# Expert activations: the high part's products with both token parts as one product of 512 columns, the two halves summed on VectorE

## The chip, the cores and the metric

The kernel runs on one core of one Trainium2 chip. The metric is the device time of one execution in microseconds (us). It computes everything in fp32 precision; where a product is large, each fp32 operand is split into a high part (rounded to the type fp32r, which TensorE multiplies in one pass) and a low part (the remainder, also as fp32r), and the product is the sum of high by high, high by low, and low by high.

## What is computed

Two blocks one after the other, each with two layers, over 256 tokens of width 1024. The second block (attention of three kinds, and a wide MLP) is not touched. The first block ends each layer with a mixture of 16384 small experts, and that is where the change lies:

```python
q = (ht @ w_q).reshape(n_tok, PEER_HEADS, PEER_QDIM)
...
gate = jax.nn.softmax(top, axis=-1)
...
u = expert_u[ec]
act = jax.nn.gelu(jnp.einsum('td,thkd->thk', hc, u), approximate=False)
return jnp.einsum('thk,thkd->td', gc * act, expert_v[ec])
```

Each token chooses 16 experts in each of 8 heads out of 128 x 128. The kernel does it densely: it goes through the experts in 128 groups of 128 (called experts 0 to 127 below, index i), computes the activation of all 256 tokens for all 128 members, applies GELU, multiplies by a table of gates that is zero where a token did not choose the member, and adds the product with `expert_v` to an accumulator that holds all tokens.

## The kernel before, in words

**One expert group i** takes these operations, all in the loop of the expert stage:

- SyncE loads `expert_u` (128x1024) and `expert_v` (128x1024), two places each, well ahead.
- ScalarE `u_high` (L1762) rounds u to its high part `utr[:, m % 2, 0]`; VectorE `u_low` (L2456) subtracts and writes the low part `utr[:, m % 2, 1]`.
- TensorE `activations` (L1207): 8 slices k of the width, 3 products each (`HALVES`, L32), 24 products of 128x128 by 128x256 into 256 columns of a PSUM bank, `prob_ps[:, m % 2]`.
- ScalarE `gelu` (L1769) reads the bank and writes `ga[:, m % 2]` (128x256).
- VectorE `weighted` (L2470, L2472, L2474) multiplies by the gate's row, rounds to `wtr` high, subtracts for `wtr` low; the semaphore `wt_ready` follows.
- ScalarE `v_high` (L1779) and VectorE `v_low` (L2481) split v in the same way into `vr`, of which there is only one buffer, so that `v_high` waits for the end of the combine before (`v_used`).
- TensorE `combine` (L1219): 12 products of 128x512, accumulated into `acc`.

**The order of the work** is written out by hand and each engine keeps to its own: TensorE does activations(i), combine(i-1), activations(i+1), combine(i). ScalarE does u_high(i+1), gelu(i), v_high(i). VectorE does u_low(i+1), weighted(i), v_low(i). Combine(i) waits for `wt_ready` and for v_low(i). `prob_ps` has two banks used in turn; activations(i) waits until the GELU of i-2 has read its bank.

**The two layers** differ. In layer 1 the first 8 groups have their activations computed earlier (`EARLY`), from plain fp32, with GELU applied then; so 120 groups go through `activations`, 128 in layer 0: 248 in all. In layer 0, beside groups 27 to 122, the kernel also computes the modulation vectors of the next layer: a loop of 12 rounds of 8 groups, where VectorE, in the first four steps of each round, adds one "ada piece" between weighted(i) and v_low(i): two multiply-adds of 128x512 (`ada_piece`, L2129, called at L2514). One product on TensorE (L1263) and one copy on ScalarE (L1596) per round belong to it. The other groups of layer 0 and all of layer 1 have plain steps.

```python
for j in range(8):
    i = it * 8 + (PLAIN + 3 + j)
    u_low(i + 1, j)
    weighted(i, (3 + j) % 4)
    if j < 4:
        ...
        ada_piece(it + ADA_START, j, next_pieces, next_sum, next_row)
    ...
    v_low(i, (3 + j) % 4)
```

Of the kernel before, what the change touches and what calls it, by code (L numbers as in the profile page):

```python
# [11 lines left out]
ALU = mybir.AluOpType  # L12
ACT = mybir.ActivationFunctionType
X = mybir.AxisListType.X

P = 128
D = 1024
S = 256
T = S // P
KD = D // P  # L20
# [9 lines left out]
NKEYS = 128  # L30
PLACES = 2
HALVES = ((0, 0), (0, 1), (1, 0))  # L32
# [26 lines left out]
EARLY = (0, 8)  # L59
# [160 lines left out]
def two_blocks(nc, io, out):  # L220
    ctx = ExitStack()
    with ctx:
        def sem(name):
            return ctx.enter_context(nc.semaphore(name))
# [6 lines left out]
        prob_ps = ctx.enter_context(nc.psum_tensor("prob_ps", [P, 2, 512], F32))  # L231
# [60 lines left out]
        ut_act = Signal(sem("ut_act"), a=NKEYS)  # L292
        ut_dve = Signal(sem("ut_dve"), a=NKEYS)
        am_full = Signal(sem("am_full"), a=NKEYS)
        gelu_done = Signal(sem("gelu_done"), a=NKEYS)
        wt_ready = Signal(sem("wt_ready"), a=NKEYS)
        v_used = Signal(sem("v_used"), a=NKEYS)
# [39 lines left out]
        with ExitStack() as second:  # L337
# [4 lines left out]
            hTr = half("hTr", [P, 2, KD, S])  # L342
            wtr = half("wtr", [P, 2, 2, S])
            half("beside_experts", [P, 4096], F32)
            utr = half("utr", [P, 2, 2, D])
# [66 lines left out]
        start = Region(arena, start_at)  # L412
# [24 lines left out]
        ga = rc.take(2, S)  # L437
# [388 lines left out]
        def _(pe):  # L826
# [168 lines left out]
            for l in range(DEPTH):  # L995
# [40 lines left out]
                for t in range(T):  # L1036
                    for k in range(KD):
                        pe.matmul(acc[:, b, t, :], hT[:, k, t * P:t * P + P], w(k, 0, 256),
                                  start=(k == 0), stop=(k == KD - 1))
                for j in range(2):  # L1040
                    ins = columns_T(acc[:, b, 2 + j, :], w, hT, 256 + j * P)
# [9 lines left out]
                for t in range(T):  # L1051
                    for k in range(KD):
                        ins = pe.matmul(acc[:, b, t, :], hT[:, k, t * P:t * P + P], w(k, 0, 256),
                                        start=(k == 0), stop=(k == KD - 1))
# [12 lines left out]
                for g in range(4):  # L1067
                    r = 64 * (g % 2)
                    for kt in range(T):
                        ins = pe.matmul(pooled[r:r + 64, g // 2, :], z[:, kt, 768 + 64 * g:832 + 64 * g],  # L1070
                                        pool_m[:, kt, g, :], start=(kt == 0), stop=(kt == 1))
# [7 lines left out]
                for g in range(4):  # L1079
                    r = 64 * (g % 2)  # L1080
                    ins = pe.matmul(pooled[r:r + 64, g // 2, :], pool_wt[r:r + 64, g // 2, :],
                                    plT[r:r + 64, g // 2, :], start=True, stop=True)
# [63 lines left out]
                if l == 0:  # L1146
                    pe.wait_ge(t5_skew, 16 * 16)
                    pe.wait_ge(t5_kept, 1)
                    for h in range(8):
                        if h >= 2:  # L1150
                            pe.wait_ge(t5_done, h - 1)
                        pe.matmul(prob_ps[:, h % 2, :], flip, skewed[:, h].rearrange("p t s -> p (t s)"),
                                  start=True, stop=False)
                        pe.matmul(prob_ps[:, h % 2, :], ident[:], causal_a, start=False, stop=True).then_inc(t5_flip, 1)
                    pe.wait_ge(t5_done, 8)
                    for s in (7, 8):
                        pe.wait_ge(bias_row_in, 16 * s)
                        pe.matmul(prob_ps[:, (s - 1) % 2], ones, bias_row, start=True, stop=False)
                        for p in range(4):
                            pe.wait_ge(piece_in[p], s * 16 + 16)  # L1160
                            for k in range(2):
                                ins = pe.matmul(prob_ps[:, (s - 1) % 2], cbc[:, 2 * p + k, :], start_pieces[:, p, k],
                                                start=False, stop=(p == 3 and k == 1))
# [3 lines left out]
                for i in range(EARLY[l]):  # L1167
# [3 lines left out]
                    for k in range(KD):  # L1171
                        ins = pe.matmul(prob_ps[:, i % 2, 0:S], early_u[:, i, k * P:k * P + P], hT[:, k, :],
                                        start=(k == 0), stop=(k == KD - 1))
# [9 lines left out]
                for n in range(S // TOKG):  # L1183
# [5 lines left out]
                    for q in range(TOKG):  # L1189
                        ins = pe.matmul(gate_ps[:, n % 2, q * P:q * P + P], rows[:, n % 2, 1, q, :], rows[:, n % 2, 0, q, :],  # L1190
                                        start=True, stop=True)
# [5 lines left out]
                def activations(i, m):  # L1197

                    pe.wait_ge(*ut_act.at("a", l, i + 1 - EARLY[l]))
                    pe.wait_ge(*ut_dve.at("a", l, i + 1 - EARLY[l]))  # L1200
                    if not (isinstance(i, int) and i < EARLY[l] + 2):
                        pe.wait_ge(*gelu_done.at("a", l, i - 1 - EARLY[l]))
                    elif EARLY[l]:
                        pe.wait_ge(early_done, EARLY[l])
                    for k in range(KD):
                        for n, (uh, hh) in enumerate(HALVES):
                            ins = pe.matmul(prob_ps[:, m % 2, 0:S], utr[:, m % 2, uh, k * P:k * P + P], hTr[:, hh, k, :],  # L1207
                                            start=(k == 0 and n == 0), stop=(k == KD - 1 and n == 2))
                    ins.then_inc(am_full.sem, 1)

                def combine(i, m, first=False, last=False):
# [39 lines left out]
                else:  # L1251
# [3 lines left out]
                    with pe.Fori(0, 12) as it:  # L1255
                        for j in range(8):
                            i = it * 8 + (PLAIN + 3 + j)
# [15 lines left out]
            for l in range(DEPTH):  # L1273
# [42 lines left out]
                for i, (a, n) in enumerate(((0, 512), (512, 256))):  # L1316
# [3 lines left out]
                    for t in range(T):  # L1320
                        for k in range(2):
                            ins = pe.matmul(dst[:, t, 0:n], cqT[:, k, t * P:t * P + P], wuq[:, k, a:a + n],
                                            start=(k == 0), stop=(k == 1))
                    ins.then_inc(accs.full_sem("b", use), 1)
                proj_nat(l, "g1", "g1")
                for i in range(2):
# [3 lines left out]
                    for t in range(T):  # L1330
                        ins = pe.matmul(dst[:, t, :], ckvT[:, t * P:t * P + P], ob[:, i, 2 * BW:3 * BW],
                                        start=True, stop=True)
# [59 lines left out]
                for n in range(GC):  # L1392
# [3 lines left out]
                    for h in range(2):  # L1396
                        pe.wait_ge(*late_lo.at("b", l, 2 * NB + 2 * n + h + 1))
                        for t in range(T):
                            for k in range(4):
                                for m, (wp, hp) in enumerate(HALVES):  # L1400
                                    ins = pe.matmul(dst[:, t, :], (hT_hi, mx_lo)[hp][:, 4 * h + k, t * P:t * P + P],  # L1401
                                                    late_operand(2 * NB + 2 * n + h, wp)[:, k, :],
                                                    start=(h == 0 and k == 0 and m == 0), stop=(h == 1 and k == 3 and m == 2))
# [4 lines left out]
                for i in range(8):  # L1408
                    use = f"up{i}"
                    pe.wait_ge(*accs.free_at("b", l, use))  # L1410
                    for h in range(2):
# [3 lines left out]
                        for j in range(2):  # L1415
                            for n, (wp, hp) in enumerate(HALVES):
                                if j == 0 and n == 2:
                                    pe.wait_ge(*mlp_lo.at("b", l, u + 1))
                                for k in range(KD):
                                    ins = pe.matmul(acc[:, accs.buf("b", use), 2 * h + j, :],  # L1420
                                                    mlp_operand(u, wp)[:, k, j * P:j * P + P], hm_r[hp][:, k, :],
                                                    start=(k == 0 and n == 0), stop=(k == KD - 1 and n == 2))
# [3 lines left out]
                for j in range(8):  # L1426
                    pe.wait_ge(*u_ready.at("b", l, j + 1))
                    for n in range(GC):
# [3 lines left out]
                        for t in range(T):  # L1432
                            for k in range(4):
                                for m, (wp, up) in enumerate(HALVES):
                                    ins = pe.matmul(dst[:, t, :], uTr[:, up, 4 * j + k, t * P:t * P + P],  # L1435
                                                    mlp_operand(u, wp)[:, k, :], start=(j == 0 and k == 0 and m == 0),
                                                    stop=(j == 7 and k == 3 and m == 2))
# [78 lines left out]
        def _(act):  # L1516
# [81 lines left out]
            for l in range(DEPTH):  # L1598
# [163 lines left out]
                    act.copy(utr[:, m % 2, 0], expert_u[:, m % 2]).then_inc(ut_act.sem, 1)  # L1762

                def gelu(i, m):
                    act.wait_ge(*am_full.at("a", l, i + 1 - EARLY[l]))
                    if not (isinstance(i, int) and i < 2):

                        act.wait_ge(*wt_ready.at("a", l, i - 1))
                    act.activation(ga[:, m % 2, :], prob_ps[:, m % 2, 0:S], ACT.Gelu).then_inc(gelu_done.sem, 1)  # L1769

                def v_high(i, m, place):

# [295 lines left out]
        def _(dve_):  # L2068
# [192 lines left out]
            for l in range(DEPTH):  # L2261
# [197 lines left out]
                def weighted(i, m):  # L2459

                    row = G[:, i, :] if isinstance(i, int) else G[:, bass.ds(i, 1), :].rearrange("p a s -> p (a s)")
                    g = ga[:, m % 2, :]
                    if isinstance(i, int) and i < EARLY[l]:
                        dve.wait_ge(early_done, i + 1)
                        if i >= 2:
                            dve.wait_ge(*v_used.at("a", l, i - 1))
                        dve.tensor_tensor(g, early[:, i], row, ALU.mult)
                    else:
                        dve.wait_ge(*gelu_done.at("a", l, i + 1 - EARLY[l]))
                        dve.tensor_tensor(g, g, row, ALU.mult)  # L2470
                    dve.drain()
                    dve.tensor_copy(wtr[:, m % 2, 0], g)  # L2472
                    dve.drain()
                    dve.tensor_tensor(wtr[:, m % 2, 1], g, wtr[:, m % 2, 0].bitcast(F32), ALU.subtract)\  # L2474
                        .then_inc(wt_ready.sem, 1)
# [387 lines left out]
```

## Time and profile before

| what | value |
|---|---|
| median of 3 runs | 3186.84 us (3182.46 to 3190.37) |
| the profiled execution, its own time | 3187.33 us |
| its span, first to last instruction | 3185.5 us |
| mean granted TensorE clock | 0.959 of full speed |
| TensorE matmul busy | 2966.0 us, 93% |
| VectorE busy | 1994.5 us, 63% |
| ScalarE busy | 1314.9 us, 41% |

Times in the profile are in us unless marked ns. PE is TensorE's matmul, PEld its weight load (which overlaps PE), DVE is VectorE, ACT is ScalarE, POOL is GpSimd. An instruction on PE is shown from its start to the end of its pipeline, so that the starts, and not the lengths, give the pace. In a timeline one line stands for successive instructions of one kind, with their number behind an x; the brackets give the engine's idle time before it and what ended that. PEclk is the clock granted to TensorE, 1.00 being its full 2.4 GHz. The span, by stage: to 379 us the front of layer 0; 379 to 1117 us its 128 expert groups; to 1455 us the front of layer 1 and its gate table; to 2156 us its expert groups; then the second block.

### The profile page before, as it was taken

Reading aid. Unit: us, or ns where it says so; the run is one execution under the profiler, and the core shown is the slowest. Engines: PE = TensorE matmul, PEld = TensorE weight load, DVE = VectorE, ACT = ScalarE, POOL = GpSimd, SP = SyncE. Lnnn points to the kernel's source line nnn. Section 1 sums busy time; section 2 is a strip of 40 time slices with the busy share of each in tenths; the row PEclk is TensorE's granted clock in tenths of the full one; section 3 lists DMA queues with packets and bytes.
Section 4 is the critical chain, followed back from the end, with each engine's and each line's share of the span. In section 5 each row is a group of like instructions: output and inputs, shape, how many; then the busy total and the mean of one; then the engine's idle time right before and its main releaser. Section 6 shows DMA issues by size and latency. Waiting matters only on the chain.

```text
span 3185.5 us, 49019 instructions
## 1 busy us (share of the span) xinstructions
PE 2966.0 (93%) x17362; PEld 2580.4 (81%) x17362; DVE 1994.5 (63%) x3639; ACT 1314.9 (41%) x2068; POOL 271.6 (9%) x387
## 2 busy tenths in 40 slices
PE   8997899999999988968999999998998898999898
PEld 4674798999999865867999999997877887978797
DVE  4659866777777633997666666665546654646564
ACT  1235843444444411575444444444433433433333
POOL 0027600000000000572000000000000000000000
PEclk9898999999999998989999999998999898999899
DMA  7532156666666631204555556554324454324354
GB/s 303 208 112 80 41 185 211 228 228 231 229 231 231 196 147 55 118 1 139 188 187 185 195 192 195 192 183 156 127 108 157 159 185 154 128 107 165 120 184 145
DMA packets 130822, 524.28 MB, mean 165 GB/s; under 512 B 17997, under 2 KB 28109, under 8 KB 108041
## 3 DMA queue, kind: packets, MB, share of 16 engines
q1 hardware_dynamic: 120664, 508.13, 46.4%
q10 hardware_dynamic: 10034, 14.52, 1.3%
q8 instruction: 75, 1.23, 0.2%
q14 instruction: 49, 0.40, 0.0%
HBM read 519.44 MB, written 3.16 MB: 164 GB/s over the span
## 4 chain that ended last, share of the span: by engine, by line
PE 77%; issue 8%; DVE 6%; ACT 6%; DVEq 1%; ACTq 1%; DMA 1%; PEld 0%; POOL 0%; PEldq 0%; SPq 0%; POOLq 0%
PE prob_ps L1207 22%; PE acc L1219 22%; PE acc L891 7%; PE acc L876 3%; PE acc L852 3%; PE acc L1420 3%; PE acc L1435 3%; PE acc L831 3%; PE acc L1376 2%; ACT arena L1745 2%; PE turn_ps L984 2%; PE acc L1401 1%; PE acc L958 1%; PE turn_ps L904 1%; ACT arena L1735 1%
## 5 line engine op out<-in xcount | busy, mean ns | idle before, releaser
L1207 PEld LDWEIGHTS prob_ps<-hTr,utr 128*128 128x128 f32 x5952 | 749.2, 192 | 33.3 <-issue 15.2
L1207 PE MATMUL prob_ps<-hTr,utr 128*128 128x256 f32 x5952 | 760.4, 284 | 8.5 <-DVE arena L2504 3.5
L1219 PE MATMUL acc<-vr,wtr 128*128 128x512 f32 x3000 | 727.5, 391 | 0.2 <-DVE vr L2481 0.2
L1219 PEld LDWEIGHTS acc<-vr,wtr 128*128 128x128 f32 x3000 | 547.5, 188 | 104.1 <-issue 0.6
L2481 DVE TENSOR_TENSOR vr<-slab,vr 128x1024 fp32r<-128x1024 f32 x250 | 306.3, 1225 | 411.7 <-ACT vr L1779 411.7
L1779 ACT CAST vr<-slab 128x1024 fp32r<-128x1024 f32 x250 | 262.4, 1050 | 580.8 <-PE acc L1219 578.1
L2456 DVE TENSOR_TENSOR utr<-slab,utr 128x1024 fp32r<-128x1024 f32 x248 | 302.0, 1218 | 14.0 <-ACT utr L1762 14.0
L1762 ACT CAST utr<-slab 128x1024 fp32r<-128x1024 f32 x248 | 259.4, 1046 | 9.3 <-issue 4.9
L2038 POOL TENSOR_TENSOR small<-small 128x2 f32<-128x2 f32 (+3 forms) x18 | 20.8, 1155 | 2753.6 <-DVE small L2110 1475.4
L2728 DVE TENSOR_TENSOR slab_lo<-slab,w_hi 128x2048 fp32r<-128x2048 f32 x64 | 143.8, 2288 | 126.7 <-ACT w_hi L2010 126.7
L1769 ACT ACTIVATE arena<-prob_ps 128x256 f32<-128x256 f32 x248 | 95.4, 385 | 224.8 <-PE prob_ps L1207 224.8
L2010 ACT CAST w_hi<-slab 128x2048 fp32r<-128x2048 f32 x64 | 119.2, 1906 | 162.2 <-DMA slab<-in_pack_b 151.5
L2545 DVE TENSOR_TENSOR slab_r<-slab,arena_r 128x2048 fp32r<-128x2048 f32 (+1 forms) x52 | 115.8, 2257 | 110.2 <-ACT arena_r L1861 86.6
L1190 PE MATMUL acc<-slab 128*128 128x128 f32 x1024 | 133.8, 286 | 40.6 <-ACT slab L1737 29.1
L1190 PEld LDWEIGHTS acc<-slab 128*128 128x128 f32 x1024 | 123.8, 198 | 50.9 <-DVE slab L2447 41.5
L852 PE MATMUL acc<-hT,slab 128*128 128x256 f32 x704 | 159.2, 386 | 1.7 <-issue 1.7
L1435 PE MATMUL acc<-w_hi,uTr 128*128 128x512 f32 x512 | 157.8, 389 | 2.3 <-issue 2.3
L2059 POOL TENSOR_SCALAR slab<-iota,arena 128x128 f32<-128x128 f32 x256 | 155.0, 622 | 43.6 <-ACT arena L1456 29.7
L2443 DVE TENSOR_SCALAR slab<-iota,arena 128x128 f32<-128x128 f32 x512 | 152.8, 367 | 3.3 <-PE acc L1190 3.1
L852 PEld LDWEIGHTS acc<-hT,slab 128*128 128x128 f32 x704 | 135.6, 194 | 22.4 <-issue 3.7
L891 PE MATMUL acc<-arena_r,hT_hi 128*128 128x512 f32 (+2 forms) x320 | 123.8, 387 | 7.2 <-DVE slab_r L2545 7.2
L891 PE MATMUL acc<-slab_r,hT_hi 128*128 128x512 f32 (+2 forms) x320 | 121.8, 381 | 0.0
(290 smaller groups left out, 4115.1 us busy)
## 6 DMA issues: line engine op xcount, KB each, us to landing
slab<-in_pack_b SPq DMA_DIRECT2D x132, 1024.0 KB, 4.9
slab<-in_peer_v SPq DMA_DIRECT2D x256, 512.0 KB, 3.5
slab<-in_peer_u SPq DMA_DIRECT2D x248, 512.0 KB, 4.6
arena<-in_pack_a SPq DMA_DIRECT2D x84, 512.0 KB, 4.7
slab<-in_pack_a SPq DMA_DIRECT2D x40, 1024.0 KB, 7.1
arena<-in_peer_u SPq DMA_DIRECT2D x4, 1024.0 KB, 13.1
slab<-in_pack_b SPq DMA_DIRECT2D x4, 832.0 KB, 5.4
arena<-in_pack_a SPq DMA_DIRECT2D x2, 1024.0 KB, 18.6
```

Of the source, the lines that this page charges most:

```text
L852: ins = pe.matmul(dst, w(k, a, P), lhs[:, k, :], start=(k == 0), stop=(k == KD - 1))
L891: ins = pe.matmul(dst[:, t, 0:n], hT_r[hp][:, 4 * h + k, t * P:t * P + P], proj_operand(u0 + h, wp)[:, k, a:a + n], start=(h == 0 and k == ...
L1190: ins = pe.matmul(gate_ps[:, n % 2, q * P:q * P + P], rows[:, n % 2, 1, q, :], rows[:, n % 2, 0, q, :], start=True, stop=True)
L1207: ins = pe.matmul(prob_ps[:, m % 2, 0:S], utr[:, m % 2, uh, k * P:k * P + P], hTr[:, hh, k, :], start=(k == 0 and n == 0), stop=(k == KD - ...
L1219: ins = pe.matmul(y_ps[:, t, n, :], wtr[:, m % 2, wh, t * P:t * P + P], v[:, vh, n * 512:n * 512 + 512], start=first and k == 0, stop=last ...
L1435: ins = pe.matmul(dst[:, t, :], uTr[:, up, 4 * j + k, t * P:t * P + P], mlp_operand(u, wp)[:, k, :], start=(j == 0 and k == 0 and m == 0), ...
L1762: act.copy(utr[:, m % 2, 0], expert_u[:, m % 2]).then_inc(ut_act.sem, 1)
L1779: act.copy(v_place(l, i)[:, 0], expert_v[:, m % 2]).then_inc(v_hi.sem, 1)
L2059: ins = nc.gpsimd.tensor_scalar(rows[:, n % 2, 1, q, :], iota[:], pairsT[:, 1, tok:tok + 1], None, ALU.is_equal)
L2443: dve.tensor_scalar(rows[:, n % 2, 0, q, :], iota[:], pairsT[:, 0, tok:tok + 1], pairsT[:, 2, tok:tok + 1], ALU.is_equal, ALU.mult)
L2456: dve.tensor_tensor(utr[:, m % 2, 1], expert_u[:, m % 2], utr[:, m % 2, 0].bitcast(F32), ALU.subtract).then_inc(ut_dve.sem, 1)
L2481: dve.tensor_tensor(v_hl[:, 1], expert_v[:, m % 2], v_hl[:, 0].bitcast(F32), ALU.subtract)\
```

## The change

In `activations`, slice by slice, the two products of u's high part (with the high and with the low part of the tokens) become one product of 512 columns, which writes both halves of the PSUM bank; the product of u's low part with the tokens' high part goes on top of the first half. So 24 products of 256 columns become 8 of 512 and 8 of 256. The activation is then the sum of the two halves, and VectorE makes it: a `tensor_reduce` at the head of `weighted`, behind u_low(i+1), reads 512 elements per partition from PSUM and writes 256 to `ga`. It waits for `am_full` and signals the new semaphore `am_summed`. GELU now waits for `am_summed`, and reads `ga` and writes it in place. Activations(i) waits for `am_summed` of i-2 in place of its GELU. GELU's wait for `wt_ready` is gone, since VectorE, which now writes `ga` first, is also its last reader.

```diff
--- before.py
+++ after.py
@@ -292,6 +292,7 @@
         ut_act = Signal(sem("ut_act"), a=NKEYS)
         ut_dve = Signal(sem("ut_dve"), a=NKEYS)
         am_full = Signal(sem("am_full"), a=NKEYS)
+        am_summed = Signal(sem("am_summed"), a=NKEYS)
         gelu_done = Signal(sem("gelu_done"), a=NKEYS)
         wt_ready = Signal(sem("wt_ready"), a=NKEYS)
         v_used = Signal(sem("v_used"), a=NKEYS)
@@ -1199,13 +1200,15 @@
                     pe.wait_ge(*ut_act.at("a", l, i + 1 - EARLY[l]))
                     pe.wait_ge(*ut_dve.at("a", l, i + 1 - EARLY[l]))
                     if not (isinstance(i, int) and i < EARLY[l] + 2):
-                        pe.wait_ge(*gelu_done.at("a", l, i - 1 - EARLY[l]))
+                        pe.wait_ge(*am_summed.at("a", l, i - 1 - EARLY[l]))
                     elif EARLY[l]:
                         pe.wait_ge(early_done, EARLY[l])
+                    both = prob_ps[:, m % 2, :].rearrange("p (h s) -> p h s", h=2)
                     for k in range(KD):
-                        for n, (uh, hh) in enumerate(HALVES):
-                            ins = pe.matmul(prob_ps[:, m % 2, 0:S], utr[:, m % 2, uh, k * P:k * P + P], hTr[:, hh, k, :],
-                                            start=(k == 0 and n == 0), stop=(k == KD - 1 and n == 2))
+                        pe.matmul(both, utr[:, m % 2, 0, k * P:k * P + P], hTr[:, :, k, :],
+                                  start=(k == 0), stop=False)
+                        ins = pe.matmul(both[:, 0], utr[:, m % 2, 1, k * P:k * P + P], hTr[:, 0, k, :],
+                                        start=False, stop=(k == KD - 1))
                     ins.then_inc(am_full.sem, 1)
 
                 def combine(i, m, first=False, last=False):
@@ -1762,11 +1765,8 @@
                     act.copy(utr[:, m % 2, 0], expert_u[:, m % 2]).then_inc(ut_act.sem, 1)
 
                 def gelu(i, m):
-                    act.wait_ge(*am_full.at("a", l, i + 1 - EARLY[l]))
-                    if not (isinstance(i, int) and i < 2):
-
-                        act.wait_ge(*wt_ready.at("a", l, i - 1))
-                    act.activation(ga[:, m % 2, :], prob_ps[:, m % 2, 0:S], ACT.Gelu).then_inc(gelu_done.sem, 1)
+                    act.wait_ge(*am_summed.at("a", l, i + 1 - EARLY[l]))
+                    act.activation(ga[:, m % 2, :], ga[:, m % 2, :], ACT.Gelu).then_inc(gelu_done.sem, 1)
 
                 def v_high(i, m, place):
 
@@ -2466,6 +2466,9 @@
                             dve.wait_ge(*v_used.at("a", l, i - 1))
                         dve.tensor_tensor(g, early[:, i], row, ALU.mult)
                     else:
+                        dve.wait_ge(*am_full.at("a", l, i + 1 - EARLY[l]))
+                        dve.tensor_reduce(g, prob_ps[:, m % 2, :].rearrange("p (h s) -> p s h", h=2), X, ALU.add)\
+                            .then_inc(am_summed.sem, 1)
                         dve.wait_ge(*gelu_done.at("a", l, i + 1 - EARLY[l]))
                         dve.tensor_tensor(g, g, row, ALU.mult)
                     dve.drain()
```

## Rows read from the trace of the kernel before

**Rows 1.** First part of the page: busy time, share of the span, instructions.

```profile
PE 2966.0 (93%) x17362; PEld 2580.4 (81%) x17362; DVE 1994.5 (63%) x3639; ACT 1314.9 (41%) x2068; POOL 271.6 (9%) x387
```

**Rows 2.** Busy time by window: length; busy (count) of PE, PEld, DVE, ACT, POOL; PEclk, DMA share, GB/s.

```profile
1387.00:1460.00 73.00, 55.35 (x427) 50.47 (x426) 68.82 (x236) 64.83 (x130) 59.99 (x101) 0.99 0.03 8
700.00:745.00 45.00, 45.00 (x288) 40.73 (x287) 32.76 (x47) 19.56 (x25) 0.00 (x0) 1.00 0.69 227
```

**Rows 3.** Timeline of one plain step: start us, length us, engine, line [idle before].

```profile
501.84 3.04 PE L1207 MATMUL prob_ps<-hTr,utr 128*128 128x256 f32 x24
502.09 1.05 ACT L1779 CAST vr<-slab 128x1024 fp32r<-128x1024 f32 x1 [2.42 <-PE acc L1219]
503.05 1.04 ACT L1762 CAST utr<-slab 128x1024 fp32r<-128x1024 f32 x1
503.17 1.23 DVE L2481 TENSOR_TENSOR vr<-slab,vr 128x1024 fp32r<-128x1024 f32 x1 [2.06 <-ACT vr L1779]
504.31 1.22 DVE L2456 TENSOR_TENSOR utr<-slab,utr 128x1024 fp32r<-128x1024 f32 x1
...
504.71 2.91 PE L1219 MATMUL acc<-vr,wtr 128*128 128x512 f32 x12
504.91 0.39 ACT L1769 ACTIVATE arena<-prob_ps 128x256 f32<-128x256 f32 x1 [0.82 <-PE prob_ps L1207]
505.45 0.42 DVE L2470 TENSOR_TENSOR arena<-arena 128x256 f32<-128x256 f32 x1
...
505.94 0.29 DVE L2472 CAST wtr<-arena 128x256 fp32r<-128x256 f32 x1
506.31 0.42 DVE L2474 TENSOR_TENSOR wtr<-arena,wtr 128x256 fp32r<-128x256 f32 x1
...
507.46 3.04 PE L1207 MATMUL prob_ps<-hTr,utr 128*128 128x256 f32 x24
```

**Rows 4.** Timeline of a step that carries an ada piece, layer 0.

```profile
774.28 0.42 DVE L2474 TENSOR_TENSOR wtr<-arena,wtr 128x256 fp32r<-128x256 f32 x1
774.62 1.57 DVE L2129 SCALAR_TENSOR_TENSOR arena<-arena,small 128x512 f32<-128x512 f32 x2
...
775.32 3.04 PE L1207 MATMUL prob_ps<-hTr,utr 128*128 128x256 f32 x24
775.58 1.05 ACT L1779 CAST vr<-slab 128x1024 fp32r<-128x1024 f32 x1 [2.42 <-PE acc L1219]
...
776.66 1.23 DVE L2481 TENSOR_TENSOR vr<-slab,vr 128x1024 fp32r<-128x1024 f32 x1 [0.47 <-ACT vr L1779]
777.81 1.22 DVE L2456 TENSOR_TENSOR utr<-slab,utr 128x1024 fp32r<-128x1024 f32 x1
```

**Rows 5.** Groups by line and shape: busy us, mean ns of one, idle before.

```profile
L1779 ACT CAST vr<-slab 128x1024 fp32r<-128x1024 f32 x250 | 262.4, 1050 | 580.8 <-PE acc L1219 578.1 <-DMA slab<-in_peer_v 2.7
...
L2169 DVE TENSOR_REDUCE small<-arena 128x4 f32<-128x1024 f32 x28 | 34.2, 1220 | 2.6
...
L1531 ACT COPY arena<-acc 128x1024 f32<-128x1024 f32 x20 | 20.3, 1013 | 66.3 <-PE acc L852 26.0 <-PE acc L876 21.8 <-PE acc L891 10.9
...
L1456 DVE COPY arena<-prob_ps 128x512 f32<-128x512 f32 x28 | 19.2, 686 | 37.8 <-PE prob_ps L969 37.8
```

**Rows 6.** Timeline: a GELU that VectorE waits for.

```profile
755.92 0.38 ACT L1769 ACTIVATE arena<-prob_ps 128x256 f32<-128x256 f32 x1 [1.67 <-PE prob_ps L1207]
...
756.44 0.43 DVE L2470 TENSOR_TENSOR arena<-arena 128x256 f32<-128x256 f32 x1 [0.76 <-ACT arena L1769]
```

**Rows 7.** Timeline: a small VectorE operation that ScalarE waits for.

```profile
2233.36 0.17 DVE L2180 TENSOR_SCALAR small<-small 128x4 f32<-128x4 f32 x1
...
2233.62 0.51 ACT L1559 ACTIVATE arena<-arena,small 128x256 f32<-128x256 f32 x1 [3.40 <-DVE small L2180]
```

**Rows 8.** Timeline: the last expert of layer 0.

```profile
1113.59 0.42 DVE L2474 TENSOR_TENSOR wtr<-arena,wtr 128x256 fp32r<-128x256 f32 x1
...
1114.61 2.88 PE L1219 MATMUL acc<-utr,wtr 128*128 128x512 f32 x12
```

## The prediction

> **What bounds the kernel now.** I read the page's first part for the engine that is full, then busy time by window to see whether it is full in the stage of the change, then the timeline of single steps there for the slack of the others. TensorE is busy 93% of the span [rows 1]. Among the expert groups it is busy all of the window at the full clock, VectorE 32.76 us of 45 [rows 2]. In a plain step [rows 3] activations(i) starts at 501.84, combine(i-1) at 504.71, activations(i+1) at 507.46: 5.62 us per group, with no gap on TensorE, while both helpers wait for it: v_high for the end of combine, and v_low for v_high after 2.06 us of idling. So in a plain step only TensorE's own work counts. A step with an ada piece is tighter [rows 4]: there VectorE ends the piece at 774.62 + 1.57 = 776.19 and idles only 0.47 us before v_low at 776.66. There are 12 rounds with 4 such steps each, 48 in all. These 0.47 us are where the change will be decided.
>
> **What TensorE saves.** 24 products of 256 columns take 504.71 - 501.84 = 2.87 us, 0.1196 each; 12 of 512 take 2.75 us, 0.2292 each [rows 3]. Twice 0.1196 less 0.2292 is 0.010 us: the part of a product's price that does not grow with its columns. The new activations cost 8 x 0.2292 + 8 x 0.1196 = 2.79 us: 0.08 us less per group, and a plain step is 5.54 us. Bounds: nothing, if a product that reads two separate runs of 256 columns is slower than the contiguous ones of combine; and 24 x 0.010 = 0.24 us, if the mixture hid the fixed part of all. I take 0.08, since both kinds of product are in the rows. The Trainium skill ("TensorE: Matmul & The Clock Gate", section "Back-to-back issue gap") puts the fixed part at some 2.5 ns per product at full clock. By it the saving would be 0.02 us per group, and the sum below 9 us higher; the rows show 10 ns, and the measurement decides.
>
> **What VectorE gets.** The reduce reads 512 elements from PSUM. Nearest row: a copy of 128x512 from PSUM, 0.686 us; a reduce of 1024 elements takes 1.22 us, no slower than a subtraction of 1024 (1.23), so a reduce pays by elements read [rows 3, 5]. I take 0.69. Bounds: 0.42, the price of 256 elements, if the output counted [rows 3], and 1.22, if the step of 256 between its two inputs halved its pace.
>
> **The wait that comes with it.** Until now GELU ran on ScalarE beside u_low, and the multiply started 1.14 us behind u_low (504.31 to 505.45) without waiting. Now VectorE must reduce, then stand idle while ScalarE does GELU, and then multiply. Hand-over VectorE to ScalarE: 2233.62 - (2233.36 + 0.17) = 0.09 us [rows 7]. GELU: 0.38 us from PSUM, and it now reads SBUF; the same ScalarE copy of 1024 elements takes 1050 ns from SBUF and 1013 from PSUM [rows 5], so 0.42. Hand-over back: 756.44 - (755.92 + 0.38) = 0.14 us [rows 6]. The multiply is late by 0.69 + 0.09 + 0.42 + 0.14 = 1.34 us. Queued behind this wait on VectorE are the rounding, the subtraction, the ada piece and v_low; combine waits for v_low. On ScalarE, v_high(i) is queued behind the later GELU, but waits for a combine anyway.
>
> **Plain steps** (counted from the start of activations(i)). u_low starts at 2.47, the reduce at 3.61, the multiply at 4.95; wtr is done at 4.95 + 0.86 + 0.42 = 6.23. v_high(i) starts 0.25 after activations(i+1), at 5.79, and ends at 6.84: v_low starts there, as before, with VectorE free since 6.2. Combine(i) is due at 5.54 + 2.79 = 8.33, v_low ends at 8.1. No stall. The cover is thin: 0.6 us on VectorE before v_low. The freed wait of GELU for `wt_ready` was long over and brings nothing; that activations(i) now waits for the reduce of i-2 costs nothing, a whole step lies between; loads stay two groups ahead. 152 groups (248 less 96) lie outside the rounds: 152 x 0.08 = 12.2 us gained.
>
> **Steps with an ada piece.** Multiply at 4.95, piece at 4.95 + 0.86 + 0.34 = 6.15, its end at 7.72, v_low at 7.79 (0.07 for the drain, the gap between the multiply's end and the rounding's start in rows 3), its end at 9.02, combine at 9.1 in place of 8.33: 0.8 us of stall. From the second on VectorE never idles and sets the pace: v_low to u_low 1.15 [rows 4], u_low to the reduce 1.14, 1.34, 0.86, 0.34 and 1.64 make 6.47 us per step in place of 5.54. So four steps stall TensorE 0.8 + 3 x 0.93 = 3.6 us; less 8 x 0.08 saved, a round is 2.9 us longer than before, twelve are 35.3 us. The other four steps of a round cannot win this back, for TensorE is what they wait for.
>
> **Edges.** At the last group of a layer combine(127) waits for wtr alone: it was ready at 1114.01 and used at 1114.61 [rows 8], so 1.34 late it costs 0.8 us, in both layers 1.6. The first group of each layer, and one group late in layer 0 behind which ScalarE issues parameter loads, have no slack in this chain: between 0 and 1.34 each, estimated 0.7, together 2.1.
>
> **Sum:** 35.3 - 12.2 + 1.6 + 2.1 = +26.8 us on the profiled execution's 3187.33, which is 0.5 above the median: 3213.6, rounded to 3213. No change to what lies behind 2156 us or before 379 us. Differences under 0.3%, 9.6 us, a measurement of this kernel can't tell from none.
>
> **Rivals.**
> - *Faster: the ada steps hold.* Place: v_low behind the ada piece. If the added 1.34 us came out under about 0.5 (0.47 of idling there, and little more before combine), no step would stall, and only TensorE's saving and part of the edges remained: 3187 - 248 x 0.08 + 3 = 3170. For it: VectorE idles 12 us of 45. Against: the idling lies behind the wait for v_high, and reduce and GELU alone are over twice 0.5 us. 8%.
> - *Same: the fixed part vanishes.* With 0.24 us saved per group, 152 x 0.24 = 36.5 us against 35.3 + 3.7: 3190. Or a cheap reduce (0.42) with a somewhat better TensorE saving. 10%.
> - *The clock falls.* TensorE would idle 0.93 of 6.47 us for four steps in a row; if the granted clock fell to 1.2 GHz for one step of each round, its 5.5 us would double, some 4 us beyond the stalls: 12 x 4 = 48, 3261. Against: in the gate stage TensorE is busy only 55.35 of 73 us, in short gaps, at a granted 0.99 [rows 2]. 3%.
> - *The wide product is no cheaper* (two runs): the 12.2 us are not gained, 3226. 10%. *The reduce takes 1.22:* the cycle is 7.0 us, a round 5.1 longer, +55: 3242. 5%.
> - The forecast itself, near 3213: 64%.
>
> **Numbers.** With the reduce at 0.42 the cycle is 6.2, a round 1.9 longer, the sum +13: 3200; a little more saving on TensorE gives the lower end, 3196. The upper end takes in the wide product without gain: 3230. Faster by over 0.3%: 0.08. Within: 0.10. Slower: 0.82.
>
> **What would show it.** Right: in the waits, TensorE's combine (the line that was L1219) waits for VectorE's v_low some 48 times with 0.8 to 0.93 us; ada steps of 6.4 to 6.5 us from activations to activations; plain steps of 5.54; VectorE's multiply waits for GELU in every step, about 0.65 us; the reduce at 0.69 us. Wrong: if combine waits for nothing in the rounds; if plain steps stall too, which a delay over 1.9 us would do; if the plain step is 5.62 or under 5.45; or if PEclk dips within the rounds.

## The result, and the profile after

The changed kernel takes 3218.27 us (median of 4 runs, 3213.38 to 3220.71) against 3188.61 (4 runs, 3182.46 to 3192.05): ratio 1.0095, 95% interval 1.0080 to 1.0109. It is slower by 29.7 us; 26.8 were worked out, and 3213 forecast with a range of 3196 to 3230.

Busy times of the page, to be held against [rows 1]:

```profile
PE 2961.4 (92%) x15378; PEld 2464.3 (77%) x15378; DVE 2153.1 (67%) x3887; ACT 1322.8 (41%) x2068; POOL 270.8 (8%) x387
```

TensorE has slightly less to do (2961.4 in place of 2966.0 us), VectorE 158.6 us more, and the span is 30.2 us longer. So the loss is waiting, not work on TensorE. The two new operations, from the groups by line and shape (busy us, mean ns of one, idle time before and what ended it):

```profile
L2470 DVE TENSOR_REDUCE arena<-prob_ps 128x256 f32<-128x512 f32 x248 | 169.6, 684 | 10.2 <-PE prob_ps L1210 8.5
...
L1769 ACT ACTIVATE arena<-arena 128x256 f32<-128x256 f32 x248 | 103.6, 418 | 566.5 <-DVE arena L2470 566.5
```

The reduce costs 684 ns and GELU from SBUF 418 ns: the terms taken were 0.69 and 0.42. Who waited for whom in the rounds (us in total, times, longest), from 560 to 1080 us of the changed kernel:

```profile
DVE arena L2473 <- ACT arena L1769: 50.6, 85, 0.6
...
DVE vr L2484 <- ACT vr L1779: 35.2, 44, 1.3
PE acc L1222 <- DVE vr L2484: 27.4, 41, 0.7
```

Before, combine waited for nothing there. Now it waits for v_low 41 times in this window (some records are missing; the sequencer's own idle time, 39.3 us on PEld, lies beside it), 0.67 us each. The forecast said 0.8 to 0.93; the view counts idle time from the end of the pipeline of the product before, and from start to start the slow steps are 0.84 to 0.93 us over a plain one. VectorE waits for GELU in all 85 steps, 0.59 us each. The step that this comes from, on VectorE, with an ada piece in it, to be read against [rows 4]:

```profile
788.75 1.23 DVE L2484 TENSOR_TENSOR vr<-slab,vr 128x1024 fp32r<-128x1024 f32 x1
789.89 1.22 DVE L2456 TENSOR_TENSOR utr<-slab,utr 128x1024 fp32r<-128x1024 f32 x1
791.03 0.68 DVE L2470 TENSOR_REDUCE arena<-prob_ps 128x256 f32<-128x512 f32 x1
792.30 0.43 DVE L2473 TENSOR_TENSOR arena<-arena 128x256 f32<-128x256 f32 x1 [0.59 <-ACT arena L1769]
792.80 0.29 DVE L2475 CAST wtr<-arena 128x256 fp32r<-128x256 f32 x1
793.17 0.43 DVE L2477 TENSOR_TENSOR wtr<-arena,wtr 128x256 fp32r<-128x256 f32 x1
793.51 1.57 DVE L2129 SCALAR_TENSOR_TENSOR arena<-arena,small 128x512 f32<-128x512 f32 x2
795.18 1.23 DVE L2484 TENSOR_TENSOR vr<-slab,vr 128x1024 fp32r<-128x1024 f32 x1
```

From v_low to v_low 6.43 us, and not one bracket but the wait for GELU: VectorE never idles otherwise. It sets the pace. Reduce to multiply is 1.27 us, the two-part ada piece 1.57, and 0.10 pass behind it. A plain step, against [rows 3] (TensorE, VectorE and ScalarE):

```profile
501.77 0.39 PE L1208 MATMUL prob_ps<-hTr,utr 128*128 128x512 f32 x1
...
502.00 0.28 PE L1210 MATMUL prob_ps<-hTr,utr 128*128 128x256 f32 x1
...
504.25 1.22 DVE L2456 TENSOR_TENSOR utr<-slab,utr 128x1024 fp32r<-128x1024 f32 x1
...
504.58 2.95 PE L1222 MATMUL acc<-vr,wtr 128*128 128x512 f32 x12
505.38 0.68 DVE L2470 TENSOR_REDUCE arena<-prob_ps 128x256 f32<-128x512 f32 x1
...
506.10 0.42 ACT L1769 ACTIVATE arena<-arena 128x256 f32<-128x256 f32 x1 [2.08 <-DVE arena L2470]
506.66 0.43 DVE L2473 TENSOR_TENSOR arena<-arena 128x256 f32<-128x256 f32 x1 [0.59 <-ACT arena L1769]
...
507.36 0.39 PE L1208 MATMUL prob_ps<-hTr,utr 128*128 128x512 f32 x1
```

Activations now take 504.58 - 501.77 = 2.81 us in place of 2.87, but combine takes 507.36 - 504.58 = 2.78 in place of 2.75. The plain step is 5.59 us: it gained 0.03, not 0.08. wtr is ready well before combine, and no plain step stalls.

Taking the starts of the activations of one group and the next over the whole trace gives the balance. Before: a plain step and a step with an ada piece 5.620 us, a round 45.81 (two of its steps carry the round's product). After: plain steps 5.593, a round 49.05, its four slow steps 6.50, 6.43, 6.45 and 6.52 (here and below rounds without the first, which is longer in every kernel). Twelve rounds: +38.8 us. The first round grew by 4.0 us (47.19 to 51.23), 0.8 more than the others, so the rounds added 39.6 in all. 152 groups by 0.027: -4.1. At the last activations of layer 1 the changed kernel is 37.8 us behind; the remaining 2.3 us are the edges, with what 370 us of unchanged code between the layers differed by. Behind that point, in code that the change does not touch, this one profiled execution took 1029.8 us and that of before 1037.4.

The first round is longer because TensorE's clock falls at its start, in both kernels. From 530 to 540 us, in two windows each (length; busy time and count of PE, PEld, DVE, ACT, POOL; PEclk, DMA share, GB/s), first before, then after:

```profile
530.00:535.00 5.00, 1.46 (x7) 1.37 (x7) 2.79 (x3) 1.99 (x2) 0.00 (x0) 0.82 0.73 277
535.00:540.00 5.00, 5.00 (x30) 4.62 (x29) 1.14 (x4) 0.39 (x1) 0.00 (x0) 0.84 0.86 345
...
530.00:535.00 5.00, 1.56 (x5) 1.38 (x6) 3.11 (x4) 1.98 (x2) 0.00 (x0) 0.76 0.73 260
535.00:540.00 5.00, 5.00 (x18) 4.17 (x16) 0.69 (x1) 0.32 (x1) 0.00 (x0) 0.55 0.85 344
```

TensorE was idle for 3.5 of the first 5 us, and the granted clock then stood at its lower level, 1.2 GHz, for part of both windows before, and for nearly all of the second in the changed kernel. From 540 us on it was 1.00 in both.

### The profile page after: what moved, and what is told of

It is laid out like the page before. It is cut to its first block, busy times and chain, and to the rows that moved or that the text cites. A ratio compares the mean times of both kernels' runs of the same rounds, so it can differ in the third digit from the quotient of the medians.

```text
span 3215.7 us, 45053 instructions
## 1 busy us (share of the span) xinstructions
PE 2961.4 (92%) x15378; PEld 2464.3 (77%) x15378; DVE 2153.1 (67%) x3887; ACT 1322.8 (41%) x2068; POOL 270.8 (8%) x387
## 4 chain that ended last, share of the span: by engine, by line
PE 66%; DVE 13%; issue 10%; ACT 7%; DVEq 2%; DMA 1%; ACTq 1%; POOL 0%; PEldq 0%; SPq 0%; POOLq 0%; PEld 0%
PE acc L1222 17%; PE prob_ps L1208 11%; PE acc L892 7%; PE prob_ps L1210 5%; PE acc L853 3%; PE acc L1423 3%; PE acc L877 3%; PE acc L1438 3%; PE acc L832 3%; PE acc L1379 2%; DVE utr L2456 2%; ACT arena L1748 2%; PE turn_ps L985 2%; DVE arena L2129 1%; PE acc L1404 1%
## 5 line engine op out<-in xcount | busy, mean ns | idle before, releaser
L1222 PE MATMUL acc<-vr,wtr 128*128 128x512 f32 x3000 | 738.7, 395 | 33.2 <-DVE vr L2484 33.2
L1208 PE MATMUL prob_ps<-hTr,utr 128*128 128x512 f32 x1984 | 716.4, 401 | 7.4 <-DVE arena L2507 3.5
L1210 PE MATMUL prob_ps<-hTr,utr 128*128 128x256 f32 x1984 | 557.9, 281 | 0.0
L1769 ACT ACTIVATE arena<-arena 128x256 f32<-128x256 f32 x248 | 103.6, 418 | 566.5 <-DVE arena L2470 566.5
L2473 DVE TENSOR_TENSOR arena<-arena 128x256 f32<-128x256 f32 x248 | 105.5, 425 | 147.3 <-ACT arena L1769 147.3
L2470 DVE TENSOR_REDUCE arena<-prob_ps 128x256 f32<-128x512 f32 x248 | 169.6, 684 | 10.2 <-PE prob_ps L1210 8.5
```

Source lines behind the costliest of these rows:

```text
L1208: pe.matmul(both, utr[:, m % 2, 0, k * P:k * P + P], hTr[:, :, k, :], start=(k == 0), stop=False)
L1210: ins = pe.matmul(both[:, 0], utr[:, m % 2, 1, k * P:k * P + P], hTr[:, 0, k, :], start=False, stop=(k == KD - 1))
L1222: ins = pe.matmul(y_ps[:, t, n, :], wtr[:, m % 2, wh, t * P:t * P + P], v[:, vh, n * 512:n * 512 + 512], start=first and k == 0, stop=last ...
L2470: dve.tensor_reduce(g, prob_ps[:, m % 2, :].rearrange("p (h s) -> p s h", h=2), X, ALU.add)\
```

## The experiments

Each is told as an edit to the kernel before or to the changed one. "Wide" is a product of 512 columns, "narrow" one of 256.

**1. The wide products alone** (edit to the kernel before):

```diff
-for n, (uh, hh) in enumerate(HALVES):
-    ins = pe.matmul(prob_ps[:, m % 2, 0:S], ...)
+pe.matmul(both, utr[:, m % 2, 0, k * P:k * P + P], hTr[:, :, k, :], start=(k == 0), stop=False)
+ins = pe.matmul(both[:, 0], utr[:, m % 2, 1, k * P:k * P + P], hTr[:, 0, k, :], start=False, ...)
```

> TensorE's half of the change alone: the wide products, but GELU reads the first half of the bank as before and VectorE sums nothing (the product of u's high part with the tokens' low part is left out of the activation). Theory (the small saving seen in the changed kernel, 5.593 us per plain step in place of 5.620, is what the wide products themselves bring): plain step 5.59, no stall in the steps with an ada piece, 248 x 0.027 = 6.7 us faster than before. Rival A (the forecast's 0.08 per group is right, and the reduce on VectorE disturbs TensorE): plain step 5.54, 20 us faster. Rival B (the stalls come from the wide products, not from VectorE): steps with an ada piece stay near 6.47.

Measured: 3180.03 against 3183.24 us, ratio 0.9988 (0.9975 to 1.0001), 3 us for 6.7 expected, on the edge of what can be told. Two starts of combine in the timeline, one group apart:

```profile
1602.40 2.95 PE L1221 MATMUL acc<-vr,wtr 128*128 128x512 f32 x12
...
1607.99 2.95 PE L1221 MATMUL acc<-vr,wtr 128*128 128x512 f32 x12
```

The step is 5.59 us (5.593 over the stage), no step of a round is longer but the two around its product, and a round is 45.53 us. So 0.027 us per group is what these products bring in this order, without any reduce beside them. Rivals A and B fall: the reduce does not disturb TensorE, and the wide products make no stall.

**2. The reduce alone** (edit to the changed kernel):

```diff
-pe.matmul(both, ...); ins = pe.matmul(both[:, 0], ...)
+for n, (uh, hh) in enumerate(HALVES):
+    ins = pe.matmul(both[:, hh], utr[:, m % 2, uh, k * P:k * P + P], hTr[:, hh, k, :], ...)
```

> VectorE's half of the change alone: 24 products of 256 columns as before, the high-by-low ones written to the second half of the bank, then the reduce and the late GELU of the change. Theory: steps with an ada piece 6.43 to 6.53 us as in the changed kernel, plain steps 5.62, in all some 5 us slower than the changed kernel, about 35 us slower than before. Rival (wide products cause the stalls): no stall, time as before.

Measured: 3213.8 us, ratio 1.0110 (1.0087 to 1.0133). Slow steps 6.49, 6.41, 6.44, 6.51, plain steps 5.620, a round 49.17. Waits from 560 to 1080 us:

```profile
DVE arena L2472 <- ACT arena L1768: 50.0, 84, 0.6
...
PE acc L1221 <- DVE vr L2483: 24.8, 41, 0.7
```

The stalls are all there without a single wide product. The loss is VectorE's part of the change. By the ratio it is 35 us slower than before, as expected. The two halves add up: 35 less the 4 of experiment 1 (by its ratio) is 31, for 30 of the whole change.

**3. Wide products first** (edit to the changed kernel):

```diff
 for k in range(KD):
     pe.matmul(both, ...)
-    ins = pe.matmul(both[:, 0], ...)
+for k in range(KD):
+    ins = pe.matmul(both[:, 0], ...)
```

> The changed kernel with the 8 wide products first and then the 8 narrow ones, in place of taking turns. Theory A (the change of width from product to product costs TensorE the rest of the forecast's saving): plain step 5.52 to 5.54 us, steps with an ada piece unchanged since VectorE sets them, some 10 us faster than the changed kernel. Theory B (the price of a product does not depend on the order): plain step 5.59, no difference.

Measured: 3210.47 us, ratio 1.0078 (1.0052 to 1.0104). TensorE's timeline in layer 1:

```profile
1602.44 1.98 PE L1208 MATMUL prob_ps<-hTr,utr 128*128 128x512 f32 x8
1604.25 1.11 PE L1211 MATMUL prob_ps<-hTr,utr 128*128 128x256 f32 x8
1605.20 2.91 PE L1223 MATMUL acc<-vr,wtr 128*128 128x512 f32 x12
1607.95 1.98 PE L1208 MATMUL prob_ps<-hTr,utr 128*128 128x512 f32 x8
```

Activations take 2.76 us and combine 2.75 as before the change; the plain step is 5.51. A wide product takes (1604.25 - 1602.44) / 8 = 0.226 us, a contiguous one of combine 0.229: reading two separate runs of 256 columns costs nothing. In the first 26 groups of layer 0 the step is less regular, 5.51 to 5.56 us with a median of 5.55, where the changed kernel has 5.593 as in layer 1. The slow steps stay (6.56, 6.43, 6.43, 6.52), as they must if VectorE sets them. So the saving forecast per group was there to be had (0.107 us in layer 1, some 0.07 in those 26 groups), but not with wide and narrow taking turns. Against the changed kernel the ratio is 0.0017 lower, 5 us, less than the 10 expected and within what the two intervals leave open; the trace's plain steps are what tells theory A from B here.

**4. The ada piece in the gap** (edit to the changed kernel): the piece moves from behind `weighted` to between the reduce and the wait for GELU.

```diff
 dve.tensor_reduce(g, ...).then_inc(am_summed.sem, 1)
+if between is not None:
+    between()                      # the ada piece of steps 0 to 3
 dve.wait_ge(*gelu_done.at("a", l, i + 1 - EARLY[l]))
```

> The changed kernel with the ada piece moved from behind the multiply and its splits to between the reduce and the multiply, where VectorE waits for GELU. Theory (a step is slow because VectorE's chain, the idle wait for GELU in it, is longer than TensorE's step): the cycle is 1.15 + 1.14 + 0.65 + 1.64 + 0.86 + 0.35 = 5.8 us in place of 6.47, a round loses some 0.3 us instead of 3.2, the kernel takes some 3190. Rival (the reduce and the piece cost by their work alone, the wait for GELU being hidden anyway): no gain over the changed kernel, 3218.

Measured: 3194.71 us, ratio 1.0032 (1.0014 to 1.0050): with the same work on every engine two thirds of the loss are gone (0.0063 of 0.0095, 20 us; by the rounds of the trace 12 x 2.42 = 29 us). VectorE's timeline of a step with a piece:

```profile
770.12 1.22 DVE L2486 TENSOR_TENSOR vr<-slab,vr 128x1024 fp32r<-128x1024 f32 x1 [0.45 <-ACT vr L1779]
771.26 1.22 DVE L2456 TENSOR_TENSOR utr<-slab,utr 128x1024 fp32r<-128x1024 f32 x1
772.39 0.68 DVE L2470 TENSOR_REDUCE arena<-prob_ps 128x256 f32<-128x512 f32 x1
773.00 1.57 DVE L2129 SCALAR_TENSOR_TENSOR arena<-arena,small 128x512 f32<-128x512 f32 x2
774.78 0.43 DVE L2475 TENSOR_TENSOR arena<-arena 128x256 f32<-128x256 f32 x1 [0.22 <-issue]
...
775.65 0.43 DVE L2479 TENSOR_TENSOR wtr<-arena,wtr 128x256 fp32r<-128x256 f32 x1
776.00 1.22 DVE L2486 TENSOR_TENSOR vr<-slab,vr 128x1024 fp32r<-128x1024 f32 x1
```

From v_low to v_low 5.88 us, and the 0.59 us of waiting for GELU have disappeared under the piece. Slow steps 5.82 to 5.95, a round 46.63. The rival falls: idling in the middle of VectorE's chain cost as much as work. The cycle came out as worked out (5.8), but a round still loses 0.8 us against before in place of the expected 0.3: each of the four steps is 0.2 to 0.35 us over a plain one. That rest is VectorE's work itself, the reduce in it.

**5. Groups of four, groups of two** (edits to the changed kernel, one run each): 4 wide, 4 narrow, and again; 2 wide, 2 narrow, and so on.

> The changed kernel with the products ordered 4 wide, 4 narrow, 4 wide, 4 narrow. Theory A (each step from a narrow to a wide product costs TensorE something, 10 ns each: 8 such steps of 5.593 when they take turns, 1 at 5.513): 2 such steps, plain step 5.52 to 5.53 us. Theory B (a long run of either kind is needed before it reaches its pace): plain step near 5.56.

> The changed kernel with the products in groups of two wide and two narrow. Theory A (10 ns per step from narrow to wide): 4 such steps, plain step 5.54 to 5.55 us. Theory B: plain step near 5.59, as when they take turns.

Activations, combine and the next activations, in groups of four (3206.01 us in all):

```profile
1601.74 1.07 PE L1209 MATMUL prob_ps<-hTr,utr 128*128 128x512 f32 x4
...
1604.52 2.93 PE L1224 MATMUL acc<-vr,wtr 128*128 128x512 f32 x12
1607.28 1.07 PE L1209 MATMUL prob_ps<-hTr,utr 128*128 128x512 f32 x4
```

and combine to combine in groups of two (3199.49 us):

```profile
1601.14 2.89 PE L1224 MATMUL acc<-vr,wtr 128*128 128x512 f32 x12
...
1606.65 1.53 PE L1224 MATMUL acc<-vr,wtr 128*128 128x512 f32 x6
```

By the medians over layer 1 the step is 5.547 us in groups of four and 5.507 in groups of two: neither what theory A gave nor what B gave. With 1, 2, 4 and 8 changes from narrow to wide the steps are 5.513, 5.547, 5.507 and 5.593 us, which no price per change explains. In the first 26 groups of layer 0 the same four orders have medians of 5.55, 5.54, 5.53 and 5.593: the ranking of the three grouped orders is not the same there, and only turn by turn stands apart in both places. What makes it slow stays open.

**6. Wide first, with the piece in the gap** (experiments 3 and 4 together), and **7. the same with the ada work spread over six steps**:

```diff
-ada_piece(it + ADA_START, j, ...)              # two multiply-adds in steps 0 to 3
+for n in ((0,), (1, 2), (3,), (4, 5), (6,), (7,))[j]:   # steps 0 to 5
+    ins = dve.scalar_tensor_tensor(next_sum, next_pieces[:, p, k], ...)
-if j == 5:                                      # TensorE: the product of the round
+if j == 7:
```

> As the run before, without the spreading: wide products first, each ada piece of two multiply-adds in the gap. Theory: VectorE's cycle of 5.82 to 5.95 us stays, so a round loses 4 x 0.35 less the first step's slack against steps of 5.51, some 1 us; 152 plain groups save 0.107 each, 16 us; a round is 1.0 less 8 x 0.107, near nothing, longer than before; edges +3: some 12 us faster than before. Rival: the rounds cost as much as in the kernel with the piece in the gap and products taking turns (0.8 us each against before), 3 to 5 us faster than before.

> The changed kernel with three edits: the 8 wide products first and then the 8 narrow; the ada work in the gap between reduce and multiply; and its 8 multiply-adds spread over six steps of a round (1, 2, 1, 2, 1, 1) in place of four (2, 2, 2, 2), the product and the copy that end a round two steps and one step later. Theory (TensorE's step is 5.51 us with wide products first; VectorE's chain with one multiply-add in the gap is 1.15 + 1.14 + 0.65 + 0.82 + 0.86 + 0.35 = 5.0 us and with two 5.8, which every other step can carry): no stall in the rounds, all 248 groups save 0.107 us, 26 us, less 3 to 4 at the edges: 3187 less 23, some 3163. Rival (something else than VectorE's chain holds combine in the rounds): steps above 5.6 remain, and it is no faster than before.

Measured: 3178.88 us, ratio 0.9978 (0.9969 to 0.9987), and 3174.91 us, ratio 0.9967 (0.9957 to 0.9976), both with the shorter plain step and both short of what was expected. In the first the rounds take 46.53 us, 0.7 more than before, as its rival said: against steps of 5.51 four steps of 5.88 lose 1.5 us, and no slack in front takes any of it. The kernel is 7 us faster than before, between the theory's 12 and the rival's 3 to 5. In the second the steps with two multiply-adds take 5.86, the others 5.52 to 5.54, and a round 45.79: "every other step can carry" two was wrong. It is 10.5 us faster than before by the ratio, for 23 expected; steps above 5.6 remain, as its rival said, and whether something other than VectorE's chain holds them is left to experiment 9.

**8. The second multiply-add behind v_low** (edit to experiment 7), since v_low was thought to be what came late:

```diff
+v_low(i, (3 + j) % 4)
+if j in (1, 3):
+    add(...)                                   # the second multiply-add of the step
```

> The kernel with wide products first and the ada work spread over six steps, changed once more: in the two steps of a round that carry two multiply-adds only the first lies in the gap, the second goes behind v_low, before the next u_low. Theory (those steps were slow, 5.86 in place of 5.51 to 5.54 us, because v_low came late, while u_low has over 1 us to spare; the work of two steps, 5.0 + 5.8 us on VectorE, fits in 2 x 5.51): no step over 5.6 us in the rounds but the two that carry the round's product on TensorE, a round some 0.6 us shorter, the kernel some 7 us faster than that one and 18 us faster than before. Rival (two multiply-adds are too much work for a step wherever they lie): the slow steps stay at 5.8, no gain.

Measured: 3172.58 us, ratio 0.9966 (0.9952 to 0.9980): no gain over experiment 7. Two steps of a round stay long, 5.93 and 5.92 us, now the ones that follow. The rival holds: what counts is the work between one v_low and the next, and moving an operation across v_low only moves it into the neighbour's cycle.

**9. One multiply-add in each of the eight steps** (edit to experiment 7), and the same with the products in groups of two:

```diff
-for n in ((0,), (1, 2), (3,), (4, 5), (6,), (7,))[j]:
+for n in (j,):
```

> The kernel with wide products first and the ada work in the gap, one multiply-add in each of the eight steps of a round (1, 1, 1, 1, 1, 1, 1, 1) in place of six steps with up to two. Theory (what held TensorE in the two-fold steps, wherever the second multiply-add lay, was that the work between one v_low and the next on VectorE was 5.8 to 5.9 us, over TensorE's 5.51; with one it is 5.0 to 5.1): no step of a round over 5.6 us but the two around the round's product, a round near 45.1 us in place of 45.8, the groups of layer 0 some 8 us shorter, about 20 us faster than before. Rival (the product at the end of a round now waits for VectorE's last multiply-add, or the reduce still delays v_low): a stall at the end of each round takes it back, no gain over the kernel with six steps, 11 us faster than before.

> The same with the products in groups of two wide and two narrow, the order that had the shortest plain step (5.507 us in place of 5.513 with all wide first, in layer 1). Theory: plain steps 5.51, time the same as its neighbour within 2 us. Rival (the order matters more beside the ada work): over 5 us apart.

Measured: 3161.02 us, ratio 0.9932 (0.9909 to 0.9954), and 3157.77, ratio 0.9922 (0.9899 to 0.9945), which the measurement can't tell apart. VectorE's timeline in a round of the first:

```profile
770.46 1.23 DVE L2487 TENSOR_TENSOR vr<-slab,vr 128x1024 fp32r<-128x1024 f32 x1 [0.41 <-ACT vr L1780]
...
772.74 0.68 DVE L2471 TENSOR_REDUCE arena<-prob_ps 128x256 f32<-128x512 f32 x1
773.34 0.74 DVE L2523 SCALAR_TENSOR_TENSOR arena<-arena,small 128x512 f32<-128x512 f32 x1
774.26 0.43 DVE L2476 TENSOR_TENSOR arena<-arena 128x256 f32<-128x256 f32 x1 [0.18 <-issue]
...
776.00 1.23 DVE L2487 TENSOR_TENSOR vr<-slab,vr 128x1024 fp32r<-128x1024 f32 x1 [0.44 <-ACT vr L1780]
```

v_low to v_low is 5.54 us, TensorE's pace, with 0.44 us of idling in front of v_low again; the multiply-add (0.74) lies in the gap that GELU leaves. Its waits from 560 to 1080 us have no line for combine on v_low any more, and none for combine's weight load, which in experiment 7 still idled 22 times there (6.2 us in all, put down to issue):

```profile
DVE vr L2487 <- ACT vr L1780: 44.1, 92, 1.0
...
DVE arena L2476 <- ACT arena L1770: 0.5, 1, 0.5
```

All steps of a round are 5.52 to 5.55 us but the two around its product (5.94 and 5.99), a round is 45.13. These two kernels compute the same as the kernel before and are faster than it, by 22 and 25 us by the ratios.

## Why the prediction was right

**The mechanism held at each link.** A reduce priced by the elements it reads: 0.684 us for 0.69. GELU from SBUF: 0.418 for 0.42. Multiply late by 1.34 by the sum, 1.27 in the trace. VectorE's cycle 6.47 by the sum, 6.43 to 6.52 measured. Experiment 2 shows that this part alone makes the loss, experiment 4 that removing the wait from the chain removes most of it, experiment 9 that no stall is left once VectorE's cycle is under TensorE's. The rivals on the other side ("the ada steps hold", "the fixed part vanishes") are out, and so is the reduce at 1.22. "The clock falls" is out as a rival, for all of 560 to 1090 us ran at a PEclk of 1.00; but its sign, a dip within the rounds, did appear at the start of the first, where the kernel before has one too, and the longer dip and what came with it cost 0.8 us. "The wide product is no cheaper" was nearer to the truth than the forecast in its size (0.027 us saved lies nearer to nothing than to 0.08), though not for its reason, two separate runs.

**Two terms were mis-sized, both in the changed kernel's favour.**
- *TensorE's saving*, 0.08 us per group. The step of the argument that failed is "since both kinds of product are in the rows": each kind was priced from a run of its own kind. Taking turns they cost more, and so does the combine behind them. Measured 0.027 (experiment 1), so 4.1 us gained in place of 12.2. The figure of the Trainium skill ("TensorE: Matmul & The Clock Gate", section "Back-to-back issue gap"), 2.5 ns per product, would have given 0.02; the page gives it for a single product by itself. But experiment 3 shows that the fixed part of a product is not as small as that here: grouped, the same products save 0.107 in layer 1, 13 ns for each of the 8 left out. The agreement is of the sum, not of its reason.
- *A round*, +35.3 us for twelve, measured +38.8, and 39.6 with the first: the first slow step loses 0.90 us (6.50 against 5.59) in place of 0.8, the other three some 0.87 in place of 0.93, and 8 x 0.08 of saving within it were 8 x 0.03.

**The edges** were put at 3.7 us, 3 of them up to the last activations, where 2.3 were left. The first group began 0.7 us later, as estimated. The end of layer 0 cost more than its 0.8: combine(127) there started 7.7 us after its activations in place of 5.6, since the split of the last v, which VectorE has ahead of its last reduce, had also waited 1.31 us for its load (0.21 before). At the end of layer 1 combine(127) started 0.45 us later, for 0.8.

**The close hit is in part luck.** By these terms the expert stages lost 38 us, 11 more than the sum of 26.8, and the medians say 29.7 (the interval allows 25 to 35). The rest of the kernel is unchanged, yet its time differs from one profiled execution to the next: from the last activations to the end 1026.2 to 1040.6 us over the thirteen profiles of this study, and 370.9 to 379.6 us in front of the first. It goes with the granted clock. The front took 370.9 us at a mean PEclk of 0.95 (experiment 2) and 379.0 at 0.92 (before); the stretch between the layers 365.7 at 0.93 (experiment 2) and 376.5 at 0.89 (experiment 4); the part behind the experts 1026.2 at 0.95 (experiment 2), 1029.8 at 0.95 (the changed kernel), 1037.4 at 0.94 (before) and 1040.6 at 0.93 (experiment 1).

The loops of the experts, which run at 0.99 to 1.00, are the steadier measure. From the first to the last activations of either layer, the two layers added, the changed kernel took 36.6 us more than the one before, that of experiment 2 43.0 more, that of experiment 3 24.0 more, and the first of experiment 9 21.7 less; the ratios say 30, 35, 25 and 22. So the last two agree, while the first two kernels, over whole runs, lost some 7 us less than in their loops, just outside the intervals (25 to 35 and 28 to 42). Whether the change has a part in that, by the clock granted to the code behind it, was not settled.

## What to carry to other kernels

Compare an added operation with the slack of the tightest step of a loop, not of the usual one: here 200 of 248 steps had room for 1.3 us, and 48 had 0.5. Where an engine sets the pace, a hand-over to another one and back costs its whole idle time unless other work is put inside it; the place of the ada work alone was worth 20 us. In the plain steps, which TensorE paces, the same wait of 0.59 us cost nothing. And what counts is the sum between two successive uses of the contended step: spread small duties one to a step. Products of one width were cheaper grouped than taking turns with another width; here that is measured for 512 and 256 columns alone.

## What the runs showed of the hardware that was not expected

Taking turns between 512 and 256 columns costs TensorE time, also afterwards: activations and combine took 2.81 + 2.78 us in place of 2.76 + 2.75 with the same products sorted by width. The order is not a simple matter of the number of changes: one, two, four and eight changes gave 5.513, 5.547, 5.507 and 5.593 us per group in layer 1, and 5.55, 5.54, 5.53 and 5.593 at the start of layer 0. A reduce over two halves of a PSUM bank with a step of 256 elements between its inputs took 684 ns for 512 elements, a contiguous copy of 512 from PSUM 686 [rows 5], and it slowed nothing on TensorE: 5.593 with it and without it. The same code behind the experts took from 1026.2 us (mean granted clock 0.95) to 1040.6 (0.93) in different executions.
